# Loading expert 1's down weights ahead of the second gather, with the pooled stores moved back

## The chip, the cores and the metric

One NeuronCore of one Trainium2 chip. The metric is device time in microseconds of one execution, the median of several runs. The engines are TensorE (PE), VectorE (DVE), ScalarE (ACT), GpSimd (POOL) and SyncE (SP); each runs its own instruction stream in order, and they meet in semaphores. SP issues most transfers, GpSimd the indirect ones (gathers and scatters of rows).

## The reference

One step of a one-layer encoder on 1024 prompt rows with 16 meta rows ahead, and 64 sample rows, all of 1024 values in float32:

```
h = x + W_out [ PoolMix(u) ; RMSNorm_head(GLA(q, k, v, alpha)) * silu(r) ]
h = h + HierMoE(RMSNorm(h))       # top-1 group of 4, then top-2 of its 8 experts
y = RMSNorm(h)

def expert_block(xb, e):
    return (silu(xb @ w_eg[e]) * (xb @ w_eu[e])) @ w_ed[e]
```

`w_eg` and `w_eu` are 1024 x 512, `w_ed` is 512 x 1024, for each of 32 experts: 2 MB each, 6 MB an expert, 192 MB in all, and every one is read. Further outputs are the GLA states and, for prompt and sample, the last 15 rows of the pooling input (`new_pool_prompt`, `new_pool_sample`: 15 x 512 each).

## The kernel before

**Mixer, 0 to about 477 us.** Nine tiles of 128 rows go through projections, pooling, GLA and the output projection. Each tile's normalised rows are stored twice to a table in HBM, `hn_rows`, one copy for each of a row's two picks. The router gives each row its experts and its rank within them.

**Experts, from about 486 us.** Expert e = 2t + b. For each one:

- GpSimd gathers up to 88 rows of `hn_rows` into a lane of SBUF (`gather`, L625). Lane 0 is in the tile `late`, lane 1 in the tile `xs`; the semaphore is `rows_in[b]`.
- VectorE turns the rows by 12 block transposes (`rows_turned`, L1278) and scales them (L1287), into `xnT` (b = 0) or `hnT` (b = 1). It does this for the next expert ahead of the current expert's silu; at the start the order is: silu of expert 0, rows of expert 1, rows of expert 2, silu of expert 1, rows of expert 3, and so on. Expert 0's rows come in a way of their own.
- TensorE runs the gate matmuls, then the up matmuls in two halves (all L1790), then the down matmuls (L1802 and L1809). They count in `pe_g`, `pe_u2` and `pe_d`.
- ScalarE takes the exponential for the silu (L874), VectorE the rest of it (L1309 to L1315), and the product becomes `hid`, the operand of the down matmuls.
- ScalarE copies the result to `ye[b]` (L879, L883), and GpSimd scatters it to HBM (L636).

`ye[1]` is the tile `hs`. The two pooled outputs, `pool_out`, are cut from that same tile: VectorE writes them there (L1298), SP stores them, and ScalarE waits for both stores (`pool_stored`, L888) before it begins with expert 1, that is before expert 1's exponential.

**Weights.** Eight blocks of 2 MB hold pieces (`GATE`, `UP`, `DOWN`) of experts. `place` says which block a piece has, and `load_piece` (issue at L503) loads it. Experts 0 and 1 have the blocks (0, 1, 2) and (3, 5, LATE); LATE is the part of the tile `late` behind lane 0. SP's list at the end of the mixer (L512 to L552) is written out by hand, each load behind the wait that frees its block. From expert 4 on `load_freed` does the same in a loop: the gate weights of expert e wait for the gate matmuls of expert e - 2 (`pe_g`), and the others likewise. All of SP's transfers are in one queue, q1 in the profile; GpSimd's are in q0. The gathers of experts 0, 1, 2 are issued one after the other, then expert 3's when expert 1's lane is free.

In the code shown, `rows_in[1]` at 16 means that expert 1's rows have landed; `pe_router` at `TILES` that the last router matmuls are done; `states_stored` that the GLA states are in HBM.

Of the kernel before, what the change touches and what calls it, by code (L numbers as in the profile page):

```python
# [187 lines left out]
def build(nc, x_all, state_pool, state_gla, norm_mix, w_in, w_gate_up, b_gate, w_pool, pool_scale, gla_norm, w_out,  # L188
# [5 lines left out]
    with ExitStack() as ctx:  # L194
# [3 lines left out]
        def sem(name):  # L198
            return ctx.enter_context(nc.semaphore(name))
# [36 lines left out]
        def place(t, b, kind):  # L236

            first = isinstance(t, int) and t == 0
            return (FIRST if first else (EVEN, ODD))[b][kind]
# [8 lines left out]
        def weights(t, b, kind):  # L248
            return blocks[place(t, b, kind)].rearrange("p (k n) -> p k n", k=KF if kind == DOWN else KD)
# [70 lines left out]
        pool_out = [hs[0:HIST, 4 * n:4 * n + 4, :].rearrange("p k n -> p (k n)") for n in range(2)]  # L320
# [97 lines left out]
        s = {n: sem(n) for n in names}  # L418
        piece_in = [sem(f"piece_in{n}") for n in range(len(blocks))]
        rows_in = [sem(f"rows_in{b}") for b in range(2)]  # L420
# [16 lines left out]
        def _(sp):  # L437
# [57 lines left out]
            def load_piece(t, b, kind):  # L495
                e = 2 * t + b
                if kind == GATE:
                    src = w_eg[bass.ds(e * D, D), :].rearrange("(p k) n -> p k n", k=KD)
                elif kind == UP:
                    src = w_eu[bass.ds(e * D, D), :].rearrange("(p k) n -> p k n", k=KD)  # L500
                else:
                    src = w_ed[bass.ds(e * FF, FF), :].rearrange("(k p) n -> p k n", p=P)
                sp.dma_start(weights(t, b, kind), src).then_inc(piece_in[place(t, b, kind)], 16)  # L503
# [27 lines left out]
            sp.wait_ge(s["hn_stored"], 16 * PICKS * TILES)  # L531
            sp.wait_ge(s["pe_half_out"], 2)
            load_piece(0, 1, UP)
            sp.wait_ge(s["pool_out_ready"], 2)
            for n, out in enumerate((pool_sample, pool_prompt)):
                sp.dma_start(out, pool_out[n]).then_inc(s["pool_stored"], 16)
            sp.wait_ge(rows_in[1], 16)
            sp.wait_ge(s["pe_router"], TILES)
            sp.wait_ge(s["states_stored"], 16 * 2 * PAIRS)
            load_piece(0, 1, DOWN)  # L540
# [1 line left out]
            load_piece(1, 0, DOWN)  # L542
            sp.wait_ge(s["pe_u2"], 2)
            load_piece(1, 1, GATE)
            sp.wait_ge(s["pe_d"], 1)
            load_piece(1, 1, UP)
            sp.wait_ge(s["pe_g"], 2)
# [1380 lines left out]
```

## Time and profile before

| | us |
|---|---|
| median of 3 runs | 1041.88 |
| lowest and highest run | 1039.87, 1043.06 |
| profiled execution, its time | 1040.4 |
| profiled execution, its span | 1038.6 |
| PE busy in the span | 995.3 (96%) |
| DVE, ACT, POOL busy | 564.6, 243.8, 105.2 |
| mean granted TensorE clock | 0.991 of full speed |
| q1 (SP's transfers) | 235.19 MB, 56.2% of 16 engines' span |
| q0 (GpSimd's transfers) | 18.06 MB, 4.6% |

The span goes from the first to the last instruction of the profiled execution; its own time is 1.8 us more. The shares of busy time are means over stages with different limits: the DMA engines are almost idle through most of the mixer and full in the expert stage. A landing time is counted from the issue of a transfer to its semaphore.

### The profile page before, as it was taken

The numbers are of one execution on the slowest core, as the hardware profiler recorded it, in microseconds if no ns is written. First come the engines' busy times: TensorE is split into PE (matmuls) and PEld (weight loads), VectorE is DVE, ScalarE is ACT, GpSimd is POOL, SyncE is SP. The second block draws the span as 40 slices with busy tenths as digits, with TensorE's granted clock in tenths as the row PEclk, the third lists the DMA queues.
The fourth block names the chain that finished last, engine by engine and source line by source line (L and its number), as shares of the span: only waits on it lengthen the run. The fifth ranks groups of instructions, "written<-read, shape, count | busy, mean of one in ns | idle before, by whom it ended". The sixth has DMA issues, their size and how long they took to land.

```text
span 1038.6 us, 33500 instructions
## 1 busy us (share of the span) xinstructions
PE 995.3 (96%) x14706; PEld 785.9 (76%) x14706; DVE 564.6 (54%) x1285; ACT 243.8 (23%) x531; POOL 105.2 (10%) x169
## 2 busy tenths in 40 slices
PE   7999999999999999999999999999999999999976
PEld 7785858585868686847787888888887787878842
DVE  2433535353544444426866666766756657566637
ACT  2352323232232323122011111111111110111125
POOL 0110101010101010101110111111111110101000
PEclk8999999999999999999999999999999999999989
DMA  9921010100010101656999999999999999999959
GB/s 313 337 95 42 1 42 0 40 0 40 0 40 0 40 0 41 243 205 237 370 362 419 421 420 422 420 425 418 424 418 419 423 414 426 414 418 420 388 190 390
DMA packets 55329, 263.22 MB, mean 253 GB/s; under 512 B 11385, under 2 KB 12985, under 8 KB 47067
## 3 DMA queue, kind: packets, MB, share of 16 engines
q1 hardware_dynamic: 44506, 235.19, 56.2%
q0 software_dynamic: 8192, 18.06, 4.6%
q10 hardware_dynamic: 2592, 9.44, 2.3%
q8 instruction: 27, 0.44, 0.2%
q14 instruction: 12, 0.09, 0.0%
HBM read 247.18 MB, written 27.19 MB: 264 GB/s over the span
## 4 chain that ended last, share of the span: by engine, by line
PE 78%; DMA 17%; DVE 3%; issue 1%; ACT 1%; SPq 0%; DVEq 0%; ACTq 0%
PE bank L1504 19%; PE bank L1790 18%; DMA arena<-in_w_ed 16%; PE bank L1622 11%; PE bank L1802 8%; PE bank L1556 6%; PE bank L1809 5%; PE bank L1490 1%; PE bank L1602 1%; DMA arena<-in_w_in 1%; PE bank L1874 1%; PE bank L1563 1%; PE bank L1619 1%; PE bank L1881 1%; PE bank L1883 1%
## 5 line engine op out<-in xcount | busy, mean ns | idle before, releaser
L1504 PE MATMUL bank<-xnT,arena 128*128 128x128 f32 x1728 | 201.4, 278 | 3.8 <-DMA arena<-in_w_in 2.5
L1504 PEld LDWEIGHTS bank<-xnT,arena 128*128 128x128 f32 x1728 | 197.1, 193 | 6.3 <-DVE late L1020 3.2
L1790 PEld LDWEIGHTS bank<-hnT,arena 128*64 128x64 f32 x4096 | 157.0, 137 | 10.3 <-issue 5.6
L1790 PE MATMUL bank<-hnT,arena 128*64 128x88 f32 x4096 | 160.1, 239 | 3.2 <-issue 1.6
L1622 PE MATMUL bank<-arena,mixT 128*128 128x512 f32 x256 | 111.7, 593 | 0.0
L1802 PE MATMUL bank<-arena,osq 128*32 128x384 f32 (+1 forms) x768 | 85.7, 487 | 8.8 <-DMA arena<-in_w_ed 8.8
L1622 PEld LDWEIGHTS bank<-arena,mixT 128*128 128x128 f32 x256 | 47.9, 190 | 57.2 <-issue 57.1
L1309 DVE TENSOR_SCALAR mixT<-mixT 128x352 f32<-128x352 f32 x32 | 14.1, 440 | 136.5 <-ACT mixT L874 136.5
L1790 PE MATMUL bank<-xnT,arena 128*64 128x88 f32 x2176 | 87.3, 239 | 0.8 <-issue 0.8
L1278 DVE STREAM_TRANSPOSE hnT<-xs 32x256 f32<-32x256 f32 x192 | 83.4, 435 | 7.5 <-DMA xs<-hn_rows,idx_i 1.3
L1790 PEld LDWEIGHTS bank<-xnT,arena 128*64 128x64 f32 x2176 | 85.0, 137 | 1.4 <-issue 1.3
L1809 PE MATMUL bank<-arena,osq 128*32 128x256 f32 (+1 forms) x384 | 85.9, 380 | 0.0
L1802 PE MATMUL bank<-arena,silu_r 128*32 128x384 f32 x720 | 80.3, 487 | 5.5 <-DMA arena<-in_w_ed 3.4
L1278 DVE STREAM_TRANSPOSE xnT<-late 32x256 f32<-32x256 f32 x180 | 78.1, 434 | 5.2
L1809 PE MATMUL bank<-arena,silu_r 128*32 128x256 f32 x360 | 80.5, 380 | 0.0
L1790 PEld LDWEIGHTS bank<-xnT,work 128*64 128x64 f32 x1920 | 73.6, 137 | 6.6 <-issue 4.1
L1790 PE MATMUL bank<-xnT,work 128*64 128x88 f32 x1920 | 76.4, 240 | 0.1
L1310 DVE RECIPROCAL mixT<-mixT 128x352 f32<-128x352 f32 x32 | 75.3, 2353 | 1.1
L1556 PE MATMUL bank<-arena,xnT 128*128 128x512 f32 x144 | 65.5, 597 | 0.0
L879 ACT ACTIVATE kz_v<-bank 88x384 f32<-88x384 f32 x32 | 13.8, 482 | 165.5 <-PE bank L1809 165.5
L1809 PEld LDWEIGHTS bank<-arena,osq 128*32 128x32 f32 (+1 forms) x384 | 40.0, 107 | 16.3
L879 ACT ACTIVATE hs<-bank 88x384 f32<-88x384 f32 x31 | 13.4, 482 | 163.4 <-PE bank L1809 163.4
(265 smaller groups left out, 1053.6 us busy)
## 6 DMA issues: line engine op xcount, KB each, us to landing
arena<-in_w_eu SPq DMA_DIRECT2D x32, 2048.0 KB, 9.1
arena<-in_w_ed SPq DMA_DIRECT2D x31, 2048.0 KB
arena<-in_w_eg SPq DMA_DIRECT2D x17, 2048.0 KB
work<-in_w_eg SPq DMA_DIRECT2D x15, 2048.0 KB
hn_rows<-hs ACTq DMA_DIRECT2D x18, 512.0 KB, 3.5
arena<-pick_rows SPq DMA_DIRECT2D x18, 512.0 KB, 9.9
arena<-in_w_in SPq DMA_DIRECT2D x4, 2048.0 KB
arena<-in_w_out SPq DMA_DIRECT2D x2, 2048.0 KB, 12.8
```

The costliest lines, as they stand in the source:

```text
L879: A(ye[b][0:BLOCK, half * OWN:(half + 1) * OWN], bank[6 + half][0:BLOCK, 0:OWN], ACT.Copy).then_inc(s["ye_ready"], 1)
L1278: ins = V.transpose(slotsT[b][q:q + TG, :, a:a + TG], by_k[:, :, q:q + TG])
L1309: moe.then(V.tensor_scalar(gs[:, 0:NH], sig[:, 0:NH], 1.0, None, ALU.add))
L1310: moe.then(V.reciprocal(gs[:, 0:NH], gs[:, 0:NH]))
L1490: last = nc.tensor.transpose(bank[r][:, k * CHUNK:(k + 1) * CHUNK], src[half(r), k, :], ident[half(r), half(r)])
L1504: last = mm(bank[n][:, m * P:(m + 1) * P], w[:, k, m * P:(m + 1) * P], xnT[:, k, :], start=k == 0, stop=k == KD - 1)
L1556: last = mm(bank[6][:, :], xnT[:, k, :], w_v_sb[:, k, :], start=k == 0, stop=k == KD - 1)
L1563: last = mm(bank[4][:, g * P:(g + 1) * P], w_pool_sb[:, g, :], pooled[:, g, :], start=True, stop=True)
L1622: return mm(out[:, :], mix[:, k, :], w_out_sb[:, n, k, :], start=k == 0, stop=k == KD - 1)
L1790: last = mm(out[q * SW:(q + 1) * SW, n * BLOCK:(n + 1) * BLOCK], w[:, k, m * P + q * SW:m * P + (q + 1) * SW], rowsT[b][:, k, :], start=k ...
L1802: last = mm(bank[6 + half][a:z, 0:OWN], tokens(k, g), wd[:, k, half * OWN:(half + 1) * OWN], start=k == 0, stop=k == KF - 1)
L1809: return mm(bank[n][STORE:STORE + z - a, c:c + REST], tokens(k, g), wd[:, k, 2 * OWN:D], start=k == 0 and c == 0, stop=k == KF - 1, skip_g ...
```

## The change

SP's list of waits and issues around expert 1's weights. The wait for `rows_in[1]` is gone. The wait for the pooled outputs and their two stores stand behind the load of expert 3's gate weights, where they stood ahead of expert 1's down weights. Nothing else differs.

```diff
@@ -531,10 +531,6 @@
             sp.wait_ge(s["hn_stored"], 16 * PICKS * TILES)
             sp.wait_ge(s["pe_half_out"], 2)
             load_piece(0, 1, UP)
-            sp.wait_ge(s["pool_out_ready"], 2)
-            for n, out in enumerate((pool_sample, pool_prompt)):
-                sp.dma_start(out, pool_out[n]).then_inc(s["pool_stored"], 16)
-            sp.wait_ge(rows_in[1], 16)
             sp.wait_ge(s["pe_router"], TILES)
             sp.wait_ge(s["states_stored"], 16 * 2 * PAIRS)
             load_piece(0, 1, DOWN)
@@ -542,6 +538,9 @@
             load_piece(1, 0, DOWN)
             sp.wait_ge(s["pe_u2"], 2)
             load_piece(1, 1, GATE)
+            sp.wait_ge(s["pool_out_ready"], 2)
+            for n, out in enumerate((pool_sample, pool_prompt)):
+                sp.dma_start(out, pool_out[n]).then_inc(s["pool_stored"], 16)
             sp.wait_ge(s["pe_d"], 1)
             load_piece(1, 1, UP)
             sp.wait_ge(s["pe_g"], 2)
```

`load_piece(t, b, kind)` loads expert 2t + b: (0, 1) is expert 1, (1, 0) expert 2, (1, 1) expert 3.

## Rows read from the trace of the kernel before

**Rows 1.** The chain of waits, 720 to 800 us: start us, us, what.

```profile
721.29 9.96 PE bank L1790 x256
736.57 9.97 PE bank L1790 x255
...
752.05 27.31 DMA arena<-in_w_ed
785.15 26.98 DMA arena<-in_w_ed
```

**Rows 2.** Stages: length, busy of each engine (instructions), PEclk, DMA share, GB/s.

```profile
570.00:740.00 170.00, 170.00 (x3670) 147.25 (x3668) 111.95 (x210) 27.91 (x69) 26.44 (x45) 1.00 1.01 421
785.00:981.00 196.00, 184.67 (x3968) 159.50 (x3969) 121.51 (x230) 30.57 (x75) 25.92 (x44) 1.00 1.01 416
486.00:494.00 8.00, 7.52 (x182) 7.13 (x182) 3.32 (x10) 0.46 (x1) 1.99 (x2) 1.00 0.92 342
494.00:497.00 3.00, 3.00 (x85) 3.00 (x80) 2.54 (x3) 0.00 (x0) 0.00 (x0) 1.00 0.35 70
497.00:522.00 25.00, 23.22 (x459) 18.93 (x457) 22.06 (x48) 4.35 (x11) 3.50 (x5) 1.00 1.01 414
522.00:527.00 5.00, 4.55 (x113) 4.19 (x111) 0.75 (x2) 0.56 (x2) 2.15 (x3) 1.00 0.83 294
```

**Rows 3.** SP's issues in order of time: start us, us, engine, line, transfer.

```profile
485.18 0.33 SPq L503 DMA_DIRECT2D arena<-in_w_eu  x1
...
488.85 0.43 SPq L536 DMA_DIRECT2D out_pool_prompt<-hs  x1
495.14 0.41 SPq L503 DMA_DIRECT2D late<-in_w_ed  x1
...
497.24 0.35 SPq L503 DMA_DIRECT2D arena<-in_w_eg  x1
502.57 0.35 SPq L503 DMA_DIRECT2D arena<-in_w_eu  x1
...
526.24 0.35 SPq L503 DMA_DIRECT2D work<-in_w_eg  x1
```

**Rows 4.** GpSimd's gathers of expert 1 and expert 3, in order of time.

```profile
487.49 1.00 POOL L625 DMA_INDIRECT xs<-hn_rows,idx_i  x1 [9.11 <-DVE idx_i L1293]
...
503.85 1.06 POOL L625 DMA_INDIRECT xs<-hn_rows,idx_i  x1 [14.06 <-DVE hnT L1278]
```

**Rows 5.** Transfers issued from 484 to 500 us: KB each, us to landing.

```profile
arena<-in_w_eu SPq DMA_DIRECT2D x1, 2048.0 KB, 9.1
late<-in_w_ed SPq DMA_DIRECT2D x1, 2048.0 KB, 7.9
...
out_pool_prompt<-hs SPq DMA_DIRECT2D x1, 30.0 KB, 6.1
xs<-hn_rows,idx_i POOLq DMA_INDIRECT x1, 7.6
```

**Rows 6.** ScalarE: the exponentials of expert 0 and expert 1.

```profile
492.45 0.46 ACT L874 ACTIVATE mixT<-bank 128x352 f32<-128x352 f32 x1 [8.96 <-PE bank L1790]
...
509.27 0.46 ACT L874 ACTIVATE mixT<-bank 128x352 f32<-128x352 f32 x1 [4.63 <-issue]
```

**Rows 7.** TensorE: expert 1's gate and up matmuls, and its first down matmuls.

```profile
504.11 9.93 PE L1790 MATMUL bank<-hnT,arena 128*64 128x88 f32 x256 [1.58 <-DVE hnT L1287]
514.24 0.89 PE L1802 MATMUL bank<-late,silu_r 128*32 128x384 f32 x5 [0.20 <-DVE silu_r L1315]
```

**Rows 8.** VectorE: expert 1's rows, and the first step of expert 1's silu.

```profile
497.50 5.55 DVE L1278 STREAM_TRANSPOSE hnT<-xs 32x256 f32<-32x256 f32 x12
...
510.43 0.34 DVE L1309 TENSOR_SCALAR mixT<-mixT 128x352 f32<-128x352 f32 x1
```

**Rows 9.** Gathers to landing: the one of 503.85, then all from 541.6 us on.

```profile
DMA to landing us min/median/max: 11.9/11.9/11.9
DMA to landing us min/median/max: 8.2/13.0/13.4
```

## The prediction

> **What bounds the kernel now.** I read the chain of waits first, at the place where the expert loop changes character [rows 1]. Up to about 745 us the chain is TensorE at one expert every 15.3 us (721.29 to 736.57). From 752 us the pieces are transfers of down weights, and two experts take 33.1 us (752.05 to 785.15), 16.55 us each. The stage windows say the same [rows 2]: from 570 to 740 TensorE is busy all of its 170 us while the DMA engines are full too (share 1.01, 421 GB/s); from 785 to 981 TensorE has 11.3 us of idle time (196 less 184.67) and the DMA engines are still full. So each expert's transfers cost more than its matmuls; the backlog grows through the first half of the loop and ends as the bound of the second half.
>
> It follows that the end time hangs on two things: when the stream of transfers last ran dry, and how much was left to move then. The same windows show two dry places. One is 494 to 497 (share 0.35), the other 522 to 527 (share 0.83, 294 GB/s). The first is the place of the change. The second comes after it, and is decisive: the next load, the gate weights of expert 4, is issued at 526.24 [rows 3] because TensorE only then has finished with the buffer. That moment belongs to TensorE, not to the DMA engines.
>
> **Part 1: the wait for the second gather goes.** Before, the up weights of expert 1 are issued at 485.18, the down weights of expert 1 only at 495.14, with those of expert 2 right behind [rows 3]. The gather of expert 1's rows is issued at 487.49 [rows 4] and lands 7.6 us later, at 495.1 [rows 5]: that is the wait removed. What stands behind it in program order (router finished, states stored) had long happened. So the down weights of expert 1 go out at about 485.6. Those of expert 2 wait for expert 0's gate matmuls, which ScalarE sees end at 492.45 [rows 6], almost 3 us ahead of 495.14. The gate weights of expert 3 come at 497.24 as before, since they wait for expert 0's up matmuls. The DMA engines are then busy without a gap; what was idle and is filled is 8 x 0.08 + 3 x 0.65 = 2.6 us [rows 2].
>
> Does that move the end? TensorE doesn't need these weights sooner: expert 1's down matmuls start at 514.24 [rows 7], and the weights landed at 495.14 + 7.9 = 503.0 [rows 5]. And the stream ran dry once more before 526.24, so work done earlier makes that second gap longer (by the same 2.6 us, or by up to the 5.1 us that 2.1 MB take at 414 GB/s) and nothing else. I cost the gain at nothing; what hides it is the dry stretch at 522 to 527. If that cover were not there, the gain would be 2.6 to 5.1 us.
>
> **Part 2: what the early load does to the gather.** The gather now moves beside a queue that doesn't run out. VectorE turns expert 1's rows from 497.50, and had no idle time before it [rows 8], so the landing at 495.1 had 2.4 us to spare. TensorE then starts expert 1 at 504.11 after 1.58 us of waiting for exactly these rows [rows 7]. So each us of the landing beyond 497.5 is a us of TensorE. The trace doesn't show this gather under a full queue, so I bound it. Below: it lands as before, 7.6 us, and costs nothing. Above: the slowest of the later gathers, 13.4 us [rows 9], would land at 500.9 and cost 3.4 us. The nearest row is the gather of expert 3, issued at 503.85 [rows 4], when three loads were queued and another transfer of the same queue followed closely (here it is the gather of expert 2): 11.9 us [rows 9]. I take it: 487.49 + 11.9 = 499.4, 1.9 us past 497.5. All of expert 1 and of what follows on TensorE moves by 1.9 us. No wait in the first half of the loop gives that back (TensorE has no gap from 570 to 740), the buffers come free 1.9 us later, the load of 526.24 goes out 1.9 us later, and so the transfers that bound the second half end 1.9 us later: **+1.9 us**.
>
> One rule of the Trainium skill speaks against this size ("DMA: Bandwidth & Descriptors", section "Queues, rings and completion order"): a DMA engine takes turns between the queues that have work, packet by packet. By that the gather, which already shared with the up weights, only loses the tail in which it had the engines to itself, some 0.8 us of it, which would double; it would land at about 495.9 and cost nothing. The 11.9 us above are more than that rule leaves room for, the 7.6 us fit it.
>
> **Part 3: the two pooled stores.** They were issued ahead of 489.3 (the second at 488.85 [rows 3]), behind one load; now they stand behind the gate weights of expert 3, and go out at about 497.6 and 498. SP loses nothing: 0.8 us of issuing before its next wait at 502.57. But ScalarE waits for these stores before the exponential of expert 1, and behind that wait stand VectorE's silu and TensorE's down matmuls. The exponential started at 509.27 [rows 6]; VectorE took its result at 510.43 [rows 8], being busy until then, so it has 0.7 us to spare. When do the stores land? The queue has by then four loads since 485.18. Moved between 486 and 494 were 8 x 342 GB/s = 2.74 MB, with the rest to 496 some 2.85 MB (the up weights and both gathers). Three more loads are 6.29 MB, together 9.14 MB, 22.1 us at 414 GB/s. A load alone landed in 7.9 us, 5.1 of them bytes, so 2.8 us are start and completion. The gather of expert 3 takes another 0.4 us or so. Gate weights of expert 3 land at 485.18 + 22.1 + 2.8 + 0.4 = 510.5. The second store landed 0.7 us after the load ahead of it (488.85 + 6.1 = 494.95 against 485.18 + 9.1 = 494.28) [rows 5]; so 511.2. With the rows 1.9 us late VectorE comes to the silu at 512.3 and needs the exponential begun by 511.9: the wait is hidden, at no cost. If the gather were not late, the exponential would end at 511.7 instead of 509.7 and the silu start 1.3 us late, and with it expert 1's down matmuls, which had only 0.2 us of wait before them [rows 7]: +1.3 us. The two don't add; the larger counts. If stores took as long as my estimate plus 2 us, the sum would be 3.3 us. Below, if they slip past the loads, it is nothing.
>
> **The sum.** max(1.9, 1.3) = +1.9 us. The profiled execution took 1040.4 us with a span of 1038.6, so 1042.3 for it; it lies 1.5 us under the median of the runs, 1041.88. Against the median: 1041.88 + 1.9 = **1043.8 us**.
>
> **The rivals.**
> (B) The gather stays under 10 us and the stores decide: +1.3, 1043.2 us. For it: 7.6 us with one load in the queue, and among the later gathers beside a full queue the fastest took 8.2 us [rows 9]. Against it: 11.9 for the one in the like position.
> (C) Faster: the gap at 494 to 497 is really gained, because the transfers bound the second half and the dry place at 522 to 527 is only a tail of some engines (share 0.83, not 0). Then the end comes 2.6 us sooner, 1039.3 us; at most 5.1 sooner, 1036.8. It decides from the point where the loads queued before 526.24 have not run out when the next is issued. Against it: 294 GB/s where the stretch before had 414, and the 30 us from 496 to 526 hold about 12 MB at that rate, and the five loads between 495.14 and 526.24 (both down pieces, then the three pieces of expert 3) are 10.5 MB.
> (D) Clearly slower: the gather takes 13.4 us or the stores land past 513, +3.4 us, 1045.3; a little more if both gathers, being neighbours in their queue, finish together.
> (E) Nothing is late: both landings are inside their slack, 1041.9.
>
> **Chances.** A 0.42, B 0.22, C 0.12, D 0.14, E 0.10. The likeliest gives the time. The range runs from 1040.3, with most of C left out, to 1046.3, D with the spread of the runs. Within 0.3% (3.1 us, about what can be told from no change) lie A, B, E, the most of C and a part of D: 0.72. Slower by more 0.17, faster by more 0.11.
>
> **What would show it.** In the changed profile: down weights of expert 1 issued near 485.6 and those of expert 2 near 492.5; no window under 0.8 between 486 and 520, and a longer one before the gate weights of expert 4; the gather of expert 1 landing about 12 us after its issue, with an idle of about 1.9 us on VectorE before the first transpose of expert 1's rows, put down to that gather; expert 1 on TensorE at about 506.0. The wait of ScalarE for the stores shows as idle time before its exponential at about 511; for B it, and not the gather, would be what VectorE waited for. The loads from expert 4 on should all be shifted by the same amount. I am wrong in kind if those loads go out no later and the second half still ends sooner (C), and wrong in size if TensorE starts expert 1 outside 504.1 to 507.5.

## The result, and the profile after

| | before | after |
|---|---|---|
| median | 1042.0 us (13 runs) | 1043.8 us (13 runs, 1042.15 to 1046.4) |
| ratio after / before | | 1.0022, 95% interval 1.0013 to 1.0032 |
| profiled execution, its time (span) | 1040.4 (1038.6) | 1046.4 (1044.6) |

The change makes the kernel slower by 0.22%, 2.3 us by the ratio (the medians differ by 1.8), more than the measurement is uncertain and less than the 0.3% at which the prediction drew its line. The median is the one forecast. The reason is not: the gather that I held for the cause isn't late, and the wait that I had priced as hidden under it is the loss. Note also that the profiled execution after is the slowest of the 13; its details show what happens, its sum is larger than the usual one.

SP's issues after (start us, us, engine, line, transfer), against [rows 3]:

```profile
486.40 0.33 SPq L503 DMA_DIRECT2D arena<-in_w_eu  x1
486.83 0.38 SPq L503 DMA_DIRECT2D late<-in_w_ed  x1
493.82 0.38 SPq L503 DMA_DIRECT2D arena<-in_w_ed  x1
498.67 0.34 SPq L503 DMA_DIRECT2D arena<-in_w_eg  x1
499.06 0.44 SPq L543 DMA_DIRECT2D out_pool_sample<-hs  x1
499.54 0.41 SPq L543 DMA_DIRECT2D out_pool_prompt<-hs  x1
504.00 0.37 SPq L503 DMA_DIRECT2D arena<-in_w_eu  x1
...
531.27 0.36 SPq L503 DMA_DIRECT2D work<-in_w_eg  x1
```

The change does what it says: expert 1's down weights follow its up weights by 0.4 us. Everything here stands 1.4 us later than before for a reason outside the change (ScalarE's first exponential of the experts comes at 493.89, against 492.45 in [rows 6]); below, that 1.4 is taken off. The load for expert 4, at 526.24 before, comes at 531.27: 5.0 us later, so 3.6 us net.

The stages after (length, busy of each engine, PEclk, DMA share, GB/s), against [rows 2]:

```profile
486.00:494.00 8.00, 7.71 (x158) 7.31 (x159) 3.73 (x15) 0.11 (x1) 1.99 (x2) 1.00 0.83 308
494.00:497.00 3.00, 3.00 (x86) 3.00 (x82) 2.58 (x2) 0.35 (x1) 0.00 (x0) 1.00 1.02 406
...
522.00:527.00 5.00, 5.00 (x95) 4.04 (x89) 2.70 (x6) 1.75 (x5) 0.00 (x0) 1.00 0.22 86
527.00:540.00 13.00, 12.71 (x274) 10.98 (x274) 7.46 (x14) 0.71 (x2) 2.15 (x3) 1.00 0.74 263
```

The hole at 494 to 497 is filled (share 0.35 before, 1.02 after), and the one at 522 to 527 has grown (0.83 before, 0.22 after). What was loaded early is waited out later; the second hole also grows because the load that ends it goes out later.

VectorE, ScalarE and TensorE at expert 1 after, against [rows 8], [rows 6] and [rows 7]; the bracket is the idle time just before and what ended it:

```profile
498.94 5.55 DVE L1277 STREAM_TRANSPOSE hnT<-xs 32x256 f32<-32x256 f32 x12
...
514.48 0.35 DVE L1308 TENSOR_SCALAR mixT<-mixT 128x352 f32<-128x352 f32 x1 [2.52 <-ACT mixT L873]
```

```profile
493.89 0.46 ACT L873 ACTIVATE mixT<-bank 128x352 f32<-128x352 f32 x1 [8.74 <-PE bank L1789]
...
513.98 0.46 ACT L873 ACTIVATE mixT<-bank 128x352 f32<-128x352 f32 x1 [7.90 <-DMA out_pool_prompt<-hs]
```

```profile
518.29 0.99 PE L1801 MATMUL bank<-late,silu_r 128*32 128x384 f32 x3 [2.82 <-DVE silu_r L1314]
...
525.07 5.36 PE L1789 MATMUL bank<-xnT,work 128*64 128x88 f32 x127
```

Read them from the bottom up. TensorE waits 2.82 us for expert 1's silu (0.20 before). VectorE, which makes it, had been idle for 2.52 us, waiting for ScalarE. ScalarE's exponential was held by the second pooled store, and by nothing else: it landed at 513.98, 14.4 us after its issue. And VectorE's first row has no bracket: expert 1's rows were there when it came for them, though the queue of loads was full.

One more row costs time. After the wait TensorE ran at half its clock, 1.2 GHz, until about 521:

```profile
516.00:519.00 3.00, 0.71 (x7) 0.49 (x11) 2.90 (x6) 0.00 (x0) 0.00 (x0) 0.79 0.99 408
519.00:520.00 1.00, 1.00 (x13) 0.76 (x9) 0.94 (x3) 0.00 (x0) 0.00 (x0) 0.50 0.96 389
```

Expert 1's down matmuls took 6.78 us (518.29 to 525.07), before 5.68 (514.24 to 519.92). So the 3.6 us at expert 4's load are, to 0.1 us, 2.6 of waiting (2.82 less 0.20) and 1.1 of longer matmuls at the lower clock.

### The profile page after: what moved, and what is told of

It reads as the page before. It is cut to its first block, busy times and chain, and to the rows that moved or that the text cites. A ratio compares the mean times of both kernels' runs of the same rounds, so it can differ in the third digit from the quotient of the medians.

```text
span 1044.6 us, 33500 instructions
## 1 busy us (share of the span) xinstructions
PE 997.0 (95%) x14706; PEld 787.4 (75%) x14706; DVE 564.3 (54%) x1285; ACT 243.7 (23%) x531; POOL 105.2 (10%) x169
## 4 chain that ended last, share of the span: by engine, by line
PE 75%; DMA 20%; DVE 2%; issue 1%; ACT 1%; SPq 0%; ACTq 0%; DVEq 0%
PE bank L1503 19%; DMA arena<-in_w_ed 18%; PE bank L1789 16%; PE bank L1621 11%; PE bank L1801 8%; PE bank L1555 6%; PE bank L1808 4%; DMA out_pool_prompt<-hs 1%; DMA arena<-in_w_in 1%; PE bank L1489 1%; PE bank L1601 1%; PE bank L1873 1%; PE bank L1562 1%; PE bank L1618 1%; PE bank L1882 1%
```

## The experiments

All ratios are against the kernel before on the same chip. Waits are those of TensorE before expert 1's down matmuls, in each run's profile.

| run | ratio (95% interval) | TensorE's wait, us |
|---|---|---|
| the change | 1.0022 (1.0013 to 1.0032) | 2.8 |
| again (the change) | 1.0022 (1.0012 to 1.0032) | 4.3 |
| early_load_only | 1.0004 (0.9993 to 1.0016) | 0.2 |
| act_wait_later | 1.0005 (0.9992 to 1.0018) | 0.2 |
| stores_only | 1.0063 (1.0048 to 1.0078) | 5.7 |
| stores_one_load_earlier | 1.0005 (0.9991 to 1.0018) | 0.2 |
| stores_one_load_later | 1.0096 (1.0078 to 1.0113) | 6.0 |
| stores_on_act_queue | 1.0001 (0.9988 to 1.0014) | 0.2 |
| busy_in_the_wait | 1.0019 (1.0007 to 1.0031) | see below |
| busy_in_the_wait_2 | 1.0022 (1.0007 to 1.0038) | see below |
| late_start_before | 1.0015 (1.0006 to 1.0024) | none |
| late_start_change | 1.0028 (1.0016 to 1.0041) | 0.9 |

**The change once more**

> The changed kernel once more, for a second profile beside the kernel before on the same chip. Theory W (the pooled stores decide): ScalarE's exponential of expert 1 waits again for the second pooled store, which lands some 27 us after the up weights of expert 1 are issued; VectorE idles 2 to 3 us before expert 1's silu, TensorE as long before expert 1's down matmuls, and its clock drops there; the time is 1.5 to 3.7 us over the kernel before. Theory G (the gather decides, as the prediction had it): VectorE idles about 1.9 us before the first transpose of expert 1's rows and nothing waits for the stores.

The same ratio. The profile again has ScalarE waiting for the second store and VectorE for ScalarE, longer than before (VectorE 3.95 us, where I had expected 2 to 3): the up weights of expert 1 were issued 0.9 us later in it (487.26), and the store landed 28.0 us after that, at 515.24; in the first profile after it was 27.6. W, by which the stores decide, holds; G, by which the gather does, falls.

**Half of the change: the early load alone**

```diff
             for n, out in enumerate((pool_sample, pool_prompt)):
                 sp.dma_start(out, pool_out[n]).then_inc(s["pool_stored"], 16)
-            sp.wait_ge(rows_in[1], 16)
```

> The wait for the second gather goes as in the change, but the pooled stores stay where they were, ahead of expert 1's down weights. Theory W: the stores land by 495, nobody waits for them, and the early load by itself costs nothing and gives nothing, because the queue runs dry again before expert 4's gate weights: within 0.7 us of the kernel before. Theory G: the gather is still late, +1.9 us. Theory C (the gap at 494 to 497 is really gained): 2.6 us faster than before.

1041.93 us against 1041.75: neither slower (G) nor 2.6 us faster (C). Its transfers issued from 484 to 500 us, with KB each and us to landing, against [rows 5]:

```profile
late<-in_w_ed SPq DMA_DIRECT2D x1, 2048.0 KB, 11.3
...
out_pool_prompt<-hs SPq DMA_DIRECT2D x1, 30.0 KB, 6.1
xs<-hn_rows,idx_i POOLq DMA_INDIRECT x1, 7.6
```

and its two stages:

```profile
494.00:497.00 3.00, 3.00 (x83) 2.95 (x78) 2.47 (x3) 0.00 (x0) 0.00 (x0) 1.00 1.04 421
...
522.00:527.00 5.00, 4.64 (x116) 4.31 (x114) 0.72 (x3) 0.57 (x2) 2.16 (x3) 1.00 0.49 143
```

The gather takes 7.6 us, to the digit what it took before. But this run is milder for it than the change: SP still waits for the pooled outputs here, so expert 1's down weights are issued at 489.44, 4.0 us behind the up weights (485.48) and 1.9 us behind the gather, and not 0.4 us behind the up weights. The gather in the change's own order is in the profiles of stores_one_load_later and busy_in_the_wait, below:

```profile
xs<-hn_rows,idx_i POOLq DMA_INDIRECT x1, 8.1
xs<-hn_rows,idx_i POOLq DMA_INDIRECT x1, 8.9
```

So it does get slower under the refilled queue, by 1 to 2 us, and lands in time all the same. The early load fills the first hole and deepens the second; expert 4's gate load goes out at 526.13 (526.24 before).

**The other half: the stores alone**

```diff
             load_piece(0, 1, UP)
-            sp.wait_ge(s["pool_out_ready"], 2)
-            for n, out in enumerate((pool_sample, pool_prompt)):
-                sp.dma_start(out, pool_out[n]).then_inc(s["pool_stored"], 16)
             sp.wait_ge(rows_in[1], 16)
...
             load_piece(1, 1, GATE)
+            sp.wait_ge(s["pool_out_ready"], 2)
+            for n, out in enumerate((pool_sample, pool_prompt)):
+                sp.dma_start(out, pool_out[n]).then_inc(s["pool_stored"], 16)
```

> The other half of the change alone: SP still waits for the second gather before expert 1's down weights, and the pooled stores go behind expert 3's gate weights. Theory W: three loads issued from 495 on stand ahead of the stores, which land near 514.3, so the exponential comes 5 us late, TensorE idles about 4.2 us before expert 1's down matmuls and loses 1.1 us more by the lower clock: 4 to 5.5 us slower than before, worse than the whole change. Theory G: the gather lands as before, so no loss at all.

6.6 us slower by the medians (1048.36 against 1041.75). Its transfers and ScalarE:

```profile
out_pool_sample<-hs SPq DMA_DIRECT2D x1, 30.0 KB, 15.5
out_pool_prompt<-hs SPq DMA_DIRECT2D x1, 30.0 KB, 17.3
```

```profile
516.55 0.46 ACT L874 ACTIVATE mixT<-bank 128x352 f32<-128x352 f32 x1 [10.74 <-DMA out_pool_prompt<-hs]
```

TensorE waits 5.65 us for the silu, and its down matmuls take 6.91 us at the lower clock (520.86 to 527.77). I had expected a landing at 514.3 and 4 to 5.5 us of loss; with everything 1.2 us later in this profile, the store is at 516.6, about 1 us later than that, and the loss is above my range. Two things follow. The whole loss sits in the stores. And the early load, worthless alone, does help here: it clears a load from ahead of the stores, so the whole change costs less than this half of it.

**Moving ScalarE's wait**

```diff
                 act.wait_ge(s["pe_d"], e + 1)
+                if first and b == 1:
+                    act.wait_ge(s["pool_stored"], 16 * 2)
                 if not first:
...
             expert(0, 0, True)
-            act.wait_ge(s["pool_stored"], 16 * 2)
             expert(0, 1, True)
```

> The change, with one thing more: ScalarE waits for the pooled stores not before expert 1's exponential but before it copies expert 1's result over them, some 10 us later. Theory W: all of the loss goes; no idle time over 0.3 us on TensorE before expert 1's down matmuls, no drop of its clock, time within 0.7 us of the kernel before. Theory G: still +1.9 us. Theory C: 2.6 us faster than before.

1041.86 us against 1041.75. The stores leave as late as in the change (499.15 for the second), and nobody minds: the exponential runs at 510.28, released by TensorE, and TensorE's wait is back at 0.21 us. That takes the loss away without touching SP's order.

```profile
510.28 0.46 ACT L873 ACTIVATE mixT<-bank 128x352 f32<-128x352 f32 x1 [4.59 <-PE bank L1790]
```

**A dose: the stores one load forward, one load back**

Forward, against the change:

```diff
             load_piece(1, 0, DOWN)
+            sp.wait_ge(s["pool_out_ready"], 2)
+            for n, out in enumerate((pool_sample, pool_prompt)):
+                sp.dma_start(out, pool_out[n]).then_inc(s["pool_stored"], 16)
             sp.wait_ge(s["pe_u2"], 2)
             load_piece(1, 1, GATE)
-            sp.wait_ge(s["pool_out_ready"], 2)
-            for n, out in enumerate((pool_sample, pool_prompt)):
-                sp.dma_start(out, pool_out[n]).then_inc(s["pool_stored"], 16)
```

Back, against the change:

```diff
             load_piece(1, 1, GATE)
-            sp.wait_ge(s["pool_out_ready"], 2)
-            for n, out in enumerate((pool_sample, pool_prompt)):
-                sp.dma_start(out, pool_out[n]).then_inc(s["pool_stored"], 16)
             sp.wait_ge(s["pe_d"], 1)
             load_piece(1, 1, UP)
+            sp.wait_ge(s["pool_out_ready"], 2)
+            for n, out in enumerate((pool_sample, pool_prompt)):
+                sp.dma_start(out, pool_out[n]).then_inc(s["pool_stored"], 16)
```

> The change with the pooled stores one load further forward: behind expert 2's down weights and ahead of expert 3's gate weights. Theory W: the stores land one load (5.1 us at 414 GB/s) earlier, at about 509 to 510, when the exponential is due at about 510.5; ScalarE waits for them less than 0.5 us, TensorE's wait before expert 1's down matmuls is back at 0.2 us, its clock stays up; time within 0.7 us of the kernel before. A theory in which the stores cost by being issued late, and not by the bytes queued ahead of them, expects little difference from the change: about +2 us, since they are issued only about 5 us earlier while ScalarE's wait for them was 8 to 9 us.

> The change with the pooled stores one load further back: behind expert 3's up weights, issued near 504.5. Theory W: they land 5 to 6 us later than in the change, near 519.5; TensorE's wait before expert 1's down matmuls grows by as much to 8 or 9 us, and the time is 7.5 to 10 us over the kernel before.

One load forward: within noise of the kernel before, and the exponential isn't held (510.63, no transfer named). If the late issue itself were the cost, 2 us would have stayed. One load back: 1051.98 against 1042.32 us, a loss of 0.96%, at the upper end of what W allowed. In that profile the second store lands 33.0 us after the up weights of expert 1 were issued (518.82 less 485.81), 5.4 more than the change's 27.6: one load's worth. TensorE's wait there is only 6.0 us, not 8 to 9, since expert 0 itself ran late in this execution, of which more below (its silu is needed 2.4 us later there).

```profile
518.82 0.46 ACT L873 ACTIVATE mixT<-bank 128x352 f32<-128x352 f32 x1 [11.14 <-DMA out_pool_prompt<-hs]
```

**Another queue**

```diff
             act.wait_ge(s["hn_stored"], 16 * PICKS * TILES)
+            act.wait_ge(s["pool_out_ready"], 2)
+            for n, out in enumerate((pool_sample, pool_prompt)):
+                act.dma_start(out, pool_out[n]).then_inc(s["pool_stored"], 16)
             expert(0, 0, True)
```

(and SP's stores taken out)

> The change, but ScalarE issues the two pooled stores itself, on its own queue, as soon as VectorE has written them (about 490), with expert 1's down weights already queued by SP. Theory W (what makes the stores late is the loads ahead of them in SP's queue): they land 5 to 9 us after their issue, before 499, though the DMA engines are as full as in the change; nothing waits, time within 0.7 us of the kernel before. If the full DMA engines themselves made the stores slow, they would still take some 14 us, land near 504, and also be in time: then the landing time tells, not the total.

```profile
late<-in_w_ed SPq DMA_DIRECT2D x1, 2048.0 KB, 14.9
...
out_pool_sample<-hs ACTq DMA_DIRECT2D x1, 30.0 KB, 5.2
out_pool_prompt<-hs ACTq DMA_DIRECT2D x1, 30.0 KB, 6.4
```

Issued at 489.33 and 489.96, with two 2 MB loads already in SP's queue, the stores land by 496.4 and overtake the down weights, which need 14.9 us to about 502. So what makes a 30 KB store slow is not the full DMA engines but the bytes ahead of it in its own queue. The Trainium skill ("DMA: Bandwidth & Descriptors", "Queues, rings and completion order") has descriptors of one queue consumed in ring order on each engine; the dose and this run agree with it.

**Keeping TensorE busy in the wait**

```diff
                 for half in range(2):
                     up(bank[4 + half], weights(t, b, UP), b, HALVES[half]).then_inc(s["pe_u2"], 1)
+                if isinstance(e, int) and e == 1:
+                    for _ in range(40):
+                        mm(bank[0][:, 0:P], ones_bf[:, :], ones_bf[:, :], start=True, stop=True)
                 loaded(DOWN)
```

> The change with 40 small matmuls (128x128 bf16, about 2.4 us) on TensorE between expert 1's up matmuls and its wait for the down matmuls' operand; their result is not used. It leaves the wait for the stores as it is and takes away the idleness. If the lower clock after the wait is a cost of its own, the granted clock stays at 1.0 from 519 to 523, expert 1's down matmuls take 5.7 us instead of 6.8, and the profile is about 1.1 us shorter there; the time is 0.5 to 1.1 us under the change's. If the wait were all of the loss, expert 1's down matmuls would start and take as in the change.

The first profile couldn't tell: TensorE's clock was low at expert 0 and everything behind it late, so that VectorE, busy until 513.18, wasn't held by an exponential that the store released at 512.55. So once more:

> The same kernel as in the run with 40 small matmuls in the wait, for another profile, since in that one TensorE's clock was low at expert 0 and the wait for the stores cost nothing. If in this one the clock is up at expert 0 and the stores are waited for: the granted clock stays at 1.0 after the wait and expert 1's down matmuls take 5.7 us, not 6.8.

Now the store was waited for (ScalarE's exponential at 513.52, idle 8.80 before it), and the clock stays up:

```profile
515.26 2.23 PE L1838 MATMUL bank<-ones_bf 128*128 128x128 bf16 x37 [0.87 <-issue]
517.83 0.52 PE L1801 MATMUL bank<-late,silu_r 128*32 128x384 f32 x3 [0.34 <-DVE silu_r L1314]
523.15 5.35 PE L1789 MATMUL bank<-xnT,work 128*64 128x88 f32 x127
```

```profile
519.00:520.00 1.00, 1.00 (x18) 0.69 (x14) 0.94 (x3) 0.00 (x0) 0.00 (x0) 1.00 0.88 352
```

Expert 1's down matmuls take 5.3 us here, 6.8 and 7.1 in the two profiles of the change, 1.5 and 1.8 more (against the 5.7 of the kernel before, 1.1 and 1.5 more). In the profile, then, the lower clock is a cost of its own. By the times it isn't seen: 1.0019 and 1.0022 against 1.0022, where I expected 0.5 to 1.1 us less. In an execution where the stores aren't late the 40 matmuls cost time themselves (some 2 us in the first profile, where the silu was done at 517.2 and the down matmuls began at 519.1, behind the last of them), and the intervals are 2.5 to 3.2 us wide; whether the clock costs as much in ordinary executions stays open.

**Moving the need instead of the landing**

```diff
+            keep_busy(44)
             for b in range(2):
                 expert(0, b)
```

> The kernel before with 44 small matmuls (128x128 bf16, 2.6 us) on TensorE ahead of expert 0's gate matmuls; their result is not used. It sets expert 0 back without touching SP's first loads or the stores. All theories: 2.6 us slower than the kernel before, as every later load is issued that much later.

> The same 44 matmuls in the changed kernel. Theory S (the stores' landing is fixed by SP's queue, so the loss is the distance from ScalarE's need to that landing): the need moves 2.6 us back and the landing does not, so TensorE's wait before expert 1's down matmuls is under 1.5 us, the clock stays up, and the time is within 1 us of the kernel before with the same 44 matmuls: 2.6 us over the kernel before. This would also be why executions in which TensorE's clock is low at expert 0 pay less for the change. If the loss were an added delay of its own, the two would add: 2.6 and 2.3, 4.9 us over the kernel before.

The matmuls cost less than I thought in the kernel before: 1.6 us (1.0015), not 2.6. The profile places the difference in expert 0 itself: its gate and up matmuls took 10.2 us behind the small matmuls and 11.0 without them (one profile each), which gives 0.8 us back. Expert 1's rows come later by the same amount as its matmuls, so the shorter wait for them (0.88 us in place of 1.58) gives nothing back. In the changed kernel TensorE's wait for the silu is down to 0.94 us and the clock stays at 1.00:

```profile
517.93 0.52 PE L1801 MATMUL bank<-late,silu_r 128*32 128x384 f32 x3 [0.94 <-DVE silu_r L1314]
```

By the times the change costs 1.3 us on top of the late start (1.0028 less 1.0015), where S asked for at most 1 and adding up would make it 2.3. The profile says S plainly; the times lie between the two, and their intervals overlap.

No version beat both kernels. The four without the wait are all at the time of the kernel before.

## Why the prediction was right in time and wrong in its step

**What bounds the kernel: right.** The end hangs on when the transfers last ran dry, and that moment is TensorE's. The early load alone moves nothing (1.0004), and the dry stretch before expert 4's gate weights takes up what the first hole gave (share 0.83, then 0.49 with the early load alone). Part 1 of the sum, nothing for the 2.1 MB moved forward, holds, and rival C is refuted: it asked for 2.6 us less.

**The gather under a full queue, +1.9 us: this is the step that failed.** I took 11.9 us from the gather of expert 3 as the nearest row. Measured: at most 9.8 in the change (issued at 489.15, its rows taken without idle time at 498.94), and 8.1 to 9.2 us in the five other profiles in which expert 1's down weights are issued right behind its up weights and the landing is shown; 6.6 to 7.6 in the four in which they come later. The early load does delay the gather by 1 to 2 us, inside the 2.4 us that it had to spare. The cost is nothing. The rule of the Trainium skill ("DMA: Bandwidth & Descriptors", "Queues, rings and completion order") that I had weighed against it, turns between queues packet by packet, gave an estimate of 8.4 us and no cost; it was the better guide, and these traces agree with it. Why expert 3's gather takes 11.9 us (10.8 to 11.9 wherever VectorE waits for it) isn't settled; a scatter follows it in its queue, which the first ones haven't, and nothing here tries that.

**The stores, +1.3 us, taken as hidden: the mechanism was right and the size was short.** With the gather on time this term decides, as rival B said (chance 0.22). My landing was 26.0 us after the up weights' issue; measured 27.6 and 28.0, and 27.1 to 28.0 in all five profiles in which this order of transfers held up the exponential. So 1.1 to 2 us were missing. The trace shows where. From the issue of the up weights to the landing, 486.40 to 513.98 in the first profile after (GB/s in 40 slices of 0.69 us):

```profile
GB/s 0 356 24 380 428 428 404 451 368 327 398 404 386 410 422 416 416 404 392 416 356 386 422 404 422 434 440 475 463 428 475 356 451 407 452 362 428 437 481 291
DMA packets 1915, 10.76 MB, mean 390 GB/s; under 512 B 271, under 2 KB 271, under 8 KB 1582
q1 hardware_dynamic: 1478, 9.63, 87.3%
```

At the 414 GB/s that I had reckoned with, 10.76 MB take just my 26.0 us, so the bytes were right; at the mean rate of 390 they take 27.6, and that mean is 387 to 390 in all five profiles. It is low at the start alone: the first four slices average 190 GB/s and cost 1.5 us against 414 (1.6 to 1.7 in the other four profiles), the other 36 average 412. I had given start and completion 2.8 us together; of the 9.63 MB that SP's queue moved, 1.2 MB belong to the load behind the stores, 2.8 us at 414 GB/s, so the completion alone took about that. The five profiles also show that the place in the queue decides, and not the time of issue: from its own issue the second store took 11.7 to 15.9 us, from the issue of the up weights always 27.1 to 28.0.

What varies the loss from one execution to the next is seen in the profiles: the landing is tied to the issue of expert 1's up weights, which waits for the last rows of the table, and the need is tied to expert 0's first matmuls. The first was 1.5 us ahead of the second in the first profile after (486.40, 487.89), with 2.8 us of wait, and 0.45 ahead in the other (487.26, 487.71), with 4.3.

**The lower clock after the wait** stood in no case: expert 1's down matmuls took 1.1 and 1.5 us more than in the kernel before.

**The sum.** 1.9 us predicted, 2.3 measured (1.4 to 3.3). It fits because one term that isn't there (1.9) was about as large as the one that is. The agreement of the number is luck. That the profiled executions lost more (3.6 us at expert 4's load in the one, and 1.3 more in the transfer-bound half of the loop, where the load that is 5.0 us late at 741.78 has become 6.3 late at 953.85) than the median is only partly explained. In 2 of 13 profiles of this study, of different kernels, TensorE's clock is at half from about 485 to 492, and ScalarE waits 11.15 us for expert 0's gate matmuls in place of 8.74, 2.4 us more:

```profile
486.00:488.00 2.00, 2.00 (x13) 2.00 (x12) 0.74 (x2) 0.00 (x0) 0.00 (x0) 0.50 0.94 229
```

(busy_in_the_wait.) Such an execution is slower with either kernel, but its need for the stores is later by the same 2.4 us, so the change costs it less. How often that happens can only be guessed from the mean granted clock that is on record for every run; such a stretch takes about 0.003 off it (0.988 in busy_in_the_wait, 0.991 in busy_in_the_wait_2). Of the 29 executions of the kernel before that go with the run again, 9 have a mean clock of 0.989 or less and took 1043.5 us on average, the other 20 took 1041.3. For the changed kernel it is 1044.4 (7 executions) and 1044.8 (5). By that split the change costs 0.9 us in the one kind and 3.4 in the other, as this account has it. It isn't proof: the mean doesn't say where the clock was low (the first profile after has 0.988 without such a stretch), and in the two runs with the late start the split goes the other way, 2.3 and 0.2 us, with 4 to 8 executions in each group.

## What to carry to other kernels

A small store put behind large loads in the same queue inherits their bytes: 30 KB took 4 to 6 us behind one load and 12 to 17 us behind two or more. Before moving one, look for who waits on its semaphore, and move that wait to the instruction that really overwrites the buffer, or give the store another engine's queue; either took the whole loss away here. And a gap in the transfers is worth closing only if the queue doesn't run dry again behind it at a moment that the computing engine sets: look for the last dry window, not the first.

## What the hardware showed that I had not expected

- A gather of up to 88 rows beside a refilled queue of 2 MB loads lands only a little later than beside one that runs out: 8.1 to 9.2 us against 6.6 to 7.6.
- Stores on ScalarE's queue land in 5.2 and 6.4 us with the DMA engines at a share of 0.89 to 1.03 (490 to 496), where the second of them at the end of SP's takes 14.4 in the change (17.3 in stores_only, where three whole loads had been queued just before).
- In the four profiles in which TensorE waited 2.8 to 6.0 us before expert 1's down matmuls with nothing to do, its granted clock fell to 1.2 GHz, while it was idle or (in the run again) 1.1 us after it had started, and some 3 us of matmuls ran at that clock. In the profiles with a wait of 0.9 us, or with small matmuls in the wait, it stayed at 2.4.
